# A two-layer decoder trunk in fp32 by split operands: layer one's running sums move from TensorE to VectorE scans

## The reference, cut to what matters

```python
D_MODEL = 2048; SEQ = 256; DEPTH = 2; N_HEADS = 16; HEAD_DIM = 128    # layer 0: stick-breaking, layer 1: MoBA

def stick_breaking_attention(q, k, v):          # for each block of 128 queries
    z = einsum('bhqd,bhkd->bhqk', qi, k) * scale
    past = key_pos[None, :] < t_idx[:, None]
    log_beta = log_sigmoid(z)
    log_1m_beta = where(past, log_sigmoid(-z), 0.0)
    tail = cumsum(log_1m_beta, axis=3, reverse=True) - log_1m_beta
    w = where(past, exp(log_beta + tail), 0.0)
    return einsum('bhqk,bhkd->bhqd', w, v)

def stick_breaking_layer(x, w_in, w_out):
    q, k, v, z = split(x @ w_in, 4)             # w_in is 2048 x 8192
    o = stick_breaking_attention(split_heads(q), split_heads(k), split_heads(v))
    return (merge_heads(o) * silu(z)) @ w_out

for i in range(DEPTH):
    y = stick_breaking_layer(...) if i < 1 else moba_layer(...)
    x = layer_norm(ALPHA * x + y, ln_g[i], ln_b[i])
    x = x + (p[i] @ w_ple[i]) * sigmoid(x @ w_ple_gate[i])
```

## Time and profile before

| | |
|---|---|
| median of 3 runs | 1138.38 us (1137.45 to 1138.42) |
| profiled execution, its own time | 1139.46 us |
| span of the profiled execution | 1137.8 us |
| PE busy | 1132.2 us (100%), 5216 matmuls |
| PE weight loads busy | 945.0 us (83%) |
| DVE busy | 754.9 us (66%), 811 instructions |
| ACT busy | 590.4 us (52%), 661 instructions |
| POOL busy | 266.0 us (23%) |
| chain that ended last | PE 90%, DVE 5%, DMA 3%, ACT 1% |

### The profile page before, as it was taken

One profiled execution on the slowest core, in us unless ns is written; L12 is line 12 of the kernel. 1 busy time (PEld: TensorE's weight loads), 2 busy tenths in 40 slices (PEclk: granted clock), 3 DMA queues, 4 the chain that ended last, 5 costly groups with the idle time before them and its releaser, 6 DMA issues.

```text
span 1137.8 us, 15463 instructions
## 1 busy us (share of the span) xinstructions
PE 1132.2 (100%) x5216; PEld 945.0 (83%) x5216; DVE 754.9 (66%) x811; ACT 590.4 (52%) x661; POOL 266.0 (23%) x539
## 2 busy tenths in 40 slices
PE   9999999999999999999999999999999999999998
PEld 8888888888888888888878888888888888888887
DVE  6665556556566566678888785557687777566863
ACT  6574556456547453455354555555455544435641
POOL 1402220330241300003437763420320312000000
PEclk9999999999999999999999999999999999999999
DMA  9876775675675686457687776765656768663671
GB/s 326 255 230 191 216 203 169 199 223 167 183 225 175 198 323 198 138 184 240 213 289 237 240 245 218 227 215 166 213 163 191 215 204 244 240 218 113 199 247 56
DMA packets 128635, 238.82 MB, mean 210 GB/s; under 512 B 14880, under 2 KB 17184, under 8 KB 128080
## 3 DMA queue, kind: packets, MB, share of 16 engines
...
q10 hardware_dynamic: 288, 0.52, 0.1%
...
## 4 chain that ended last, share of the span: by engine, by line
PE 90%; DVE 5%; DMA 3%; ACT 1%; issue 1%; POOL 1%; ACTq 0%; SPq 0%; DVEq 0%; POOLq 0%
PE acc L1240 28%; PE acc L1242 27%; PE acc L1241 27%; DMA raw<-in_w_ple_gate 2%; PE aux L1277 2%; DVE w_lo L772 2%; PE acc L1219 1%; PE aux L1303 1%; PE aux L1270 1%; DVE stage L967 1%; POOL stage L446 1%; DMA stage<-v_or_z 0%; DVE big L1006 0%; DVE v_or_z L1003 0%; DVE act L787 0%
## 5 line engine op out<-in xcount | busy, mean ns | idle before, releaser
L772 DVE TENSOR_TENSOR w_lo<-raw,w_hi 128x1024 fp32r<-128x1024 f32 x388 | 469.3, 1222 | 317.1 <-ACT w_hi L499 316.5
L499 ACT ACTIVATE w_hi<-raw 128x1024 fp32r<-128x1024 f32 x388 | 409.7, 1059 | 442.7 <-PE acc L1242 358.2
L1240 PE MATMUL acc<-w_hi,act 128*128 128x512 f32 x1532 | 600.3, 392 | 0.9 <-DVE act L787 0.8
L1242 PE MATMUL acc<-w_hi,act 128*128 128x512 f32 x1532 | 596.7, 389 | 0.0
L1241 PE MATMUL acc<-w_lo,act 128*128 128x512 f32 x1532 | 596.3, 389 | 0.0
L1242 PEld LDWEIGHTS acc<-w_hi,act 128*128 128x128 f32 x1532 | 287.6, 188 | 60.7
L1240 PEld LDWEIGHTS acc<-w_hi,act 128*128 128x128 f32 x1532 | 287.7, 188 | 60.2 <-DVE act L787 1.9
L1241 PEld LDWEIGHTS acc<-w_lo,act 128*128 128x128 f32 x1532 | 287.9, 188 | 58.2
L446 POOL DMA_DIRECT2D heads<-big x192 | 94.0, 498 | 274.8 <-DVE big L793 231.7
L446 POOL DMA_DIRECT2D heads<-heads x128 | 63.5, 504 | 129.0 <-DVE heads L1158 121.0
L446 POOL DMA_DIRECT2D heads<-v_or_z x64 | 31.3, 498 | 51.9 <-DVE v_or_z L793 39.1
...
## 6 DMA issues: line engine op xcount, KB each, us to landing
...
```

The lines of the kernel that those rows point to most:

```text
L499: nc.scalar.activation(w_hi[:, r], raw[:, r % RAWS], ACT.Copy).then_inc(hi_ready, 1)
L772: nc.vector.tensor_tensor(w_lo[:, r], raw[:, r % RAWS], w_hi[:, r].bitcast(F32), ALU.subtract) \
L1240: nc.tensor.matmul(dst, hi, w_hi[:, r, i], start=begin, stop=False)
L1242: mm = nc.tensor.matmul(dst, lo, w_hi[:, r, i], start=False, stop=end)
```

## The change

In layer one the scores get queries in the partitions (the roles of `q_parts` and `k_parts` are swapped, `kT_x` is read in squares for the fp32 product), as in layer two. `cumulate`, its constants and the split of softplus are gone. DVE adds the mask to the scores at once, behind each `key_scores`; `softplus` keeps its first instruction; new is `sum_later_keys`: a scan backwards over the 768 columns of a pair, restarted at each row by a zero in `segments`, and a subtraction from the scores. After Exp, `turn_weights` transposes the squares of the weights, POOL exchanges them, and `stick_weights_hi` and `stick_weights_lo` split what arrives, at slot 4 of the next chunk. PE weighs both pairs behind piece 6 of that chunk, and the gating moves behind it: pieces 0 and 1 of the chunk after, or 8 and 9 of the output projection. In the first q chunk of layer two, `last_x2_hi` goes from behind the split of slot 3 to behind that of slot 2, `last_x2_lo` from behind to in front of the split of slot 3, and `find_shift(1)` from slot 2 to slot 3. The warm-up matmuls go from 9 to 10.

```diff
-WARM_UPS = 9
+WARM_UPS = 10
...
+        segments = sb("segments", [2 * SC], BF16)
...
         def _(pool):
...
-            pool.wait_ge(consts_done, 7)
+            pool.wait_ge(consts_done, 6)
+            for first in (0, T):
+                nc.gpsimd.memset(segments[:, first::SC], 0.0).then_inc(consts_done, 1)
...
             for g in range(G):
                 exchange(chunk_evac, g * 4 + 1, qT_flat, qn, q_moved)
                 exchange(chunk_evac, g * 4 + 2, kT_flat, kn, k_moved)
+                exchange(w_turned, g + 1, w_moved_to, w_turned_to, w_moved, PW)
                 exchange(chunk_evac, g * 4 + 4, gt_flat, zn, z_moved)
...
         def _(act):
             def k_copies(k):
                 act.wait_ge(k_moved, k * MOVED + MOVED)
-                nc.scalar.activation(by_square(k_own), kT_x[:, 1::TT], ACT.Copy).then_inc(kT_ready, 1)
-                nc.scalar.activation(by_square(k_parts[:, 0]), kT_x[:, 0::TT], ACT.Copy).then_inc(k_hi, 1)
+                nc.scalar.activation(by_square(k_parts[:, 0]), kT_x, ACT.Copy).then_inc(k_hi, 1)
...
             def stick_weights_hi(k, b):
-                act.wait_ge(w_ready, k * 2 + (b + 1))
-                act.wait_ge(cum_ready, k * 2 + 2)
-                nc.scalar.activation(w_parts[:, 0, b], prob[:, b, :, 0:T], ACT.Copy).then_inc(weights_hi, 1)
+                act.wait_ge(w_moved, k * MOVED + MOVED)
+                nc.scalar.activation(early_keys(w_parts, 0, b), weights_moved_x[:, 4 * b:4 * b + 4], ACT.Copy) \
+                    .then_inc(weights_hi, 1)
...
             def exp_abs(k, b):
-                act.wait_ge(scores_ready, k * 2 + (b + 1))
+                act.wait_ge(masked, k * 2 + (b + 1))
...
             def stick_weights(k, b):
-                act.wait_ge(masked, k * 2 + (b + 1))
-                nc.scalar.activation(prob[:, b], scores_of(b), ACT.Exp).then_inc(w_ready, 1)
+                act.wait_ge(stick_log, k * 2 + (b + 1))
+                nc.scalar.activation(prob[:, b], prob[:, b], ACT.Exp).then_inc(w_ready, 1)
...
             def after_z(k):
-                return {0: [lambda: softplus_hi(k, 0)], 1: [lambda: softplus_hi(k, 1)],
-                        5: [lambda: stick_weights(k, 0)],
-                        6: [lambda: stick_weights(k, 1), lambda: stick_weights_hi(k, 0)],
-                        7: [lambda: stick_weights_hi(k, 1)]}
+                return {1: [lambda: stick_weights(k, 0)], 2: [lambda: stick_weights(k, 1)]}
             def gate_group(k):
-                return {5: [lambda: silu_z_group(k)], 6: [lambda: gated_hi(k, k)]}
+                return {4: [lambda: stick_weights_hi(k, 0), lambda: stick_weights_hi(k, 1)],
+                        5: [lambda: silu_z_group(k)]}
...
-            pieces(N_Q, N_Q, {3: [last_x2_hi, lambda: normalise_x2(0)]})
+            pieces(N_Q, N_Q, {2: [last_x2_hi], 3: [lambda: normalise_x2(0)]})
...
         def _(dve):
+            def sum_later_keys(k, b):
+                backwards = prob[:, b].rearrange("p h c -> p (h c)")[:, ::-1]
                 dve.wait_ge(sp_raw, k * 2 + (b + 1))
-                for h in range(2):
-                    diagonal = prob[:, b, h].rearrange("p (s c) -> p s c", c=P)[:, 0:3:2]
-                    last = nc.vector.tensor_tensor(diagonal, diagonal,
-                                                   past[:, :].unsqueeze(1).broadcast_to((P, 2, P)), ALU.mult)
-                last.then_inc(sp_ready, 1)
+                nc.vector.tensor_tensor_scan(backwards, segments[:, :], backwards, 0.0, ALU.mult, ALU.add) \
+                    .then_inc(sp_summed, 1)
+                dve.wait_ge(sp_summed, k * 2 + (b + 1))
+                nc.vector.tensor_tensor(prob[:, b], scores_of(b), prob[:, b], ALU.subtract).then_inc(stick_log, 1)
...
             def v_steps(k, n):
-                return {7: [lambda: values_lo(k), lambda: evacuate_v(n, 0, vn_a), lambda: softplus(k, 0)]}
+                return {6: [lambda: mask_stick(k, 0)],
+                        7: [lambda: mask_stick(k, 1), lambda: values_lo(k), lambda: evacuate_v(n, 0, vn_a),
+                            lambda: softplus(k, 0)]}
...
             def z_steps(k, n):
-                return {0: [lambda: softplus(k, 1)], 1: [lambda: softplus_lo(k, 0)], 2: [lambda: softplus_lo(k, 1)],
-                        4: [lambda: mask_stick(k, 0)], 5: [lambda: mask_stick(k, 1)],
-                        6: [lambda: stick_weights_lo(k, 0)],
-                        7: [lambda: turn_squares(n + PC, 1, zn), lambda: stick_weights_lo(k, 1)]}
+                return {0: [lambda: softplus(k, 1), lambda: sum_later_keys(k, 0)], 1: [lambda: sum_later_keys(k, 1)],
+                        2: [lambda: turn(0)], 3: [lambda: turn(1)],
+                        7: [lambda: turn_squares(n + PC, 1, zn)]}
             def gate_steps(k):
-                return {5: [lambda: gate_group(k, k, sz_a)], 6: [lambda: gated_lo(k, k, k + S_OUT[0])]}
+                return {4: [lambda: stick_weights_lo(k, 0), lambda: stick_weights_lo(k, 1)]}
+            def gate_end(k, j):
+                return {j: [lambda: gate_group(k, k, sz_a)], j + 1: [lambda: gated_lo(k, k, k + S_OUT[0])]}
...
-            out_ple_gate(0, gate_steps(G - 1))
+            out_ple_gate(0, gate_steps(G - 1) | gate_end(G - 1, 8))
...
-            pieces(N_Q, N_Q, {2: [lambda: find_shift(1)], 3: [last_x2_lo, lambda: normalise_x2(0)],
-                              4: [lambda: turn_normed(0)]} | q_end(0, 0), before={0: [lambda: x2_lo(G - 2)]})
+            pieces(N_Q, N_Q, {3: [lambda: find_shift(1), lambda: normalise_x2(0)],
+                              4: [lambda: turn_normed(0)]} | q_end(0, 0), before={0: [lambda: x2_lo(G - 2)], 3: [last_x2_lo]})
...
         def _(pe):
             def key_scores(k, b):
...
-                    three_passes(s[:, 0:T], lambda i, h=h: k_parts[:, i, h], lambda i, h=h: q_parts[:, i, h], True)
-                    mm = nc.tensor.matmul(s[:, T:SC], k_own[:, h], q_scaled[:, h, P:T], start=False, stop=True,
-                                          skip_group_check=True)
+                    nc.tensor.matmul(s[:, 0:P], q_scaled[:, h, 0:P], kT_x[:, TT * h], start=True, stop=True,
+                                     skip_group_check=True)
+                    mm = three_passes(s[:, P:SC], lambda i, h=h: q_parts[:, i, h], lambda i, h=h: k_parts[:, i, h], False)
...
-            def after_z(k):
-                return {4: [lambda: cumulate(k, 0)], 5: [lambda: cumulate(k, 1)]}
             def weigh_step(k, v_chunk):
-                return {0: [lambda: weigh_values(k, 0, v_chunk)],
-                        1: [lambda: weigh_values(k, 1, v_chunk)]}
+                return {6: [lambda: weigh_values(k, 0, v_chunk, v_parts, vn_a, w_parts, weights_moved_x),
+                            lambda: weigh_values(k, 1, v_chunk, v_parts, vn_a, w_parts, weights_moved_x)]}
...
```

133 lines of the change are left out of this document (51 added, 82 removed).

## The result

| | before | changed |
|---|---|---|
| median of 6 runs each, in turn | 1138.4 us (1137.16 to 1139.43) | 1132.07 us (1131.4 to 1134.18) |
| profiled execution, its own time | 1139.46 us | 1133.29 us |
| span of the profiled execution | 1137.8 us | 1131.5 us |

The ratio is 0.9949, with a 95% interval of 0.9939 to 0.996. The changed kernel is faster by some 6.3 us. Forecast were 10.7, and 1132.07 lies above the range of 1126.3 to 1131.0.

A forecast was written before the change was run, and what follows sets the result against it. PE was taken as the bound nearly everywhere, busy 1132.2 of 1137.8 us. The terms -9.5, -0.2, -0.3, -1.1, +0.2 and +0.2 sum to -10.7 us, giving 1127.7 us from the median, range 1126.3 to 1131.0.

The forecast's parts named there:

- The chain of the weights: Layer one, second group, from log_1p through scan, transposes and exchange to the weights' split: done before PE needs them.
- 2.7 us to spare: At weigh_values: the weights' split ends 2.7 us before PE needs it, or 4.6 with the short scan.
- about 8 us of the 16.6 covered: DVE's greatest lag, at its split of slot 3: about 8 us, within 16.6 of cover, so weights' pieces stay ahead.
- `cumulate` and scores: Layer one: removing cumulate from eight pairs gains 9.5 us; scores with the fp32 product first gain 0.2.
- Both pairs weighed in one place: Layer one's weighing, four groups: 2.36 us together instead of 2.44 apart, gaining 0.3 us.
- The last quarter: Last quarter of x2, layer two's first q chunk: last_x2_lo ends earlier, PE's wait before piece 6 goes, gaining 1.1 us.
- The last group's gating: Moved to slots 8 and 9 of the output projection, its operand comes just then at piece 12: costs 0.2 us.
- The tenth warm-up: At the start: one more warm-up matmul delays the first real one, partly regained; costs 0.2 us, ends -0.1 and +0.4.
- The scan: DVE's backward sum over a pair's 768 columns: between 0.95 and 1.9 us, taken as 1.9.
- B: Rival, weights a little late: PE waits in each of four groups, up to 1.9 us late gives 1130 to 1135; 13%.
- D: Rival, slower: PE waits at weigh_values 3.3 us in each group, needing a chain 6 us longer; 4%.
- A: The forecast case: PE never waits for the weights and terms hold, -11.3 to -9 us; 72%.

The follow-up runs named there:

- quarter_only: The kernel before with only the edits around the last quarter of x2 (last_x2_hi, last_x2_lo, find_shift(1) moved): 1138.08 us, ratio 0.9997.
- warm9: The changed kernel with nine warm-up matmuls instead of ten: 1132.44 us, ratio 0.9946.
- two_scans: The changed kernel with each scan done twice, so its sums are wrong: 1152.44 us, ratio 1.0122.
- weigh7: The changed kernel with weigh_values of layer one behind piece 7 instead of piece 6: 1128.97 us, ratio 0.9928.
- front_of_four: The changed kernel with the weights split in slot 3, in front of slot 4's split instead of behind it: 1128.89 us, ratio 0.9927.
- weigh7_table: The changed kernel weighing behind piece 7, with the table for Exp loaded ahead of the last group's v chunk: 1128.35 us, ratio 0.9915.
- short_sum: The changed kernel with one ordinary product in place of each scan, leaving out the sum: 1129.22 us, ratio 0.9916.
- no_exchange: The changed kernel without the weights' 16 DMAs a group, the transposed squares split where they lie: 1128.05 us, ratio 0.9909.
- matrix_thirteen: The changed kernel with the output projection's first 16 pieces loaded from w_in_a instead of w_out_a, values wrong: 1130.35 us, ratio 0.9932.

## Why the prediction was wrong in size, point by point

The direction and the mechanism held, and one step failed. It is the last one of "The chain of the weights": "from the end of the transposes ... to the end of `probs_lo` takes 16.05 us", and with it "**2.7 us to spare**". It took 22.4 us in the last group and 21.0 in the second, for which it was worked out. There the way up to the transposes was right: they end at 185.91, 19.9 us ahead of 205.85, where 18.75 had been forecast. The 16.05 from layer two was measured where ACT and DVE are level with PE. Here their splits are behind, and the weights' split is queued behind the split of slot 4. I had worked out that very lag ("about 8 us of the 16.6 covered") and found it harmless. It is harmless to PE's pieces, which have eight slots of cover; the row of L1242 confirms that with 0.0 us. It is not to a step that hangs on a slot, which has no such cover. Its spare time is what lies between its own slot and its consumer: 5.5 us, less 3.0 for the splits. The last paragraph of the prediction had this sign in its list ("ACT at slot 4 waiting for DMA by more than the splits are ahead"), and it is what the trace shows: ACT waited 1.46 us for a load in front of that split.

Behind that stood an assumption that I didn't write down: that 19 us are enough to make the lag up. By the durations of their splits, 1.06 and 1.22 us a piece, ACT and DVE could do it. The loads can't, because four buffers stop them while ACT stands, and then they share full DMA engines with two exchanges.

- *`cumulate` and scores* (-9.5, -0.2): right. 2.45 us a group in three, 2.17 in the last: 9.52 against 9.7. Of the two, `cumulate` brought more than forecast (2.49 a group instead of 2.38), and the scores brought nothing: the v chunk takes 24.09 us instead of 24.05.
- *Both pairs weighed in one place* (-0.3): -0.08 in groups one and three, as worked out. In the other two the wait lay on top.
- *The last quarter* (-1.1): -1.14, and by itself too.
- *The last group's gating* (+0.2): +0.21.
- *The tenth warm-up* (+0.2): not to be read from one trace. PE's second chunk starts at 28.22 before and at 27.42 in the changed kernel's profile, 0.8 earlier. But quarter_only, with nine and no edit there, starts it at 27.62, and warm9 at 27.57. The eleven traces with ten lie between 27.24 and 28.34. So the start-up scatters by 0.65 us with nine and by 1.1 with ten, and one trace of each says nothing of a term of 0.2.
- *The scan* (1.9, bounds 0.95 and 1.9): 1.75, inside. The transposes ended 18.9 us ahead of `weigh_values` in the last group and 19.9 in the others, against 18.75.
- *Not in the sum at all*: the wait of 3.02 in the last group and 0.5 in the second, 1.67 us at a lower clock, and 0.28 for keys. Together some 5.5 us. Against the forecast stands a start-up that was 1.0 better in this trace. That the traces' difference of 6.3 us is also that of the medians is partly luck: the profiled execution of before, with its late start, lies 1.1 us above its median, and the changed kernel's, with its loss of clock, 1.2 above its own.

**The rivals.** B, "weights a little late", had the range (1130 to 1135) and named "DMAs that land later than in layer two". It deserved more than 13%: I gave the chance by the 2.7 us to spare, which was the wrong number. It also had the wait in each of four groups, while it was nearly all in the last. D's mechanism is real, as two_scans shows with 1152.44, but its threshold is lower than I said. 3.5 us more a group are enough to go from 6 us faster to 14 slower, where I had put the crossing at 6 us more, since my spare time was too large and the clock wasn't in it. A was the forecast, and its time is what weigh7 (1128.97), front_of_four (1128.89) and weigh7_table (1128.35) show: the sum is right for the kernel without that wait.

**Settled**: the loss is at `weigh_values` of the last group, and it comes from the weights' split standing behind a late slot (front_of_four, weigh7). The slot is late since the splits' lag isn't made up, to which the scan's time (short_sum, two_scans), the exchange's load on the DMA engines (no_exchange) and the matrix (matrix_thirteen) each contribute. That the masks, for which ACT also stands, add to it is not tested. **Open**: how much each contributes, for they act through the same lag and are not additive, and the place scatters by 1 us. Open too is why the keys make the last group's v chunk 0.2 to 0.8 us longer in every variant but no_exchange. POOL starts their exchange 2.3 us behind the transpose it needs, and the trace names no releaser.
